# Channel mixing: five row blocks of 3, 3, 3, 4 and 4 tiles instead of four of 4, 4, 4 and 5

## What is computed

```python
    h2 = modulate(rms_norm(x), sh2, sc2)
    ff = jnp.square(jax.nn.relu(h2 @ w_up)) @ w_down
    x = x + g2[:, None, :] * ff
```

## Time and profile before

| | us |
|---|---|
| median of 3 runs | 3468.93 (3468.54 to 3474.66) |
| the profiled execution | 3469.96 |
| its span, first to last instruction | 3468.5 |
| stages ahead of channel mixing | up to 1902 |
| channel mixing, first block with its start | 1902 to 2274.6 |
| second, third block | 348.2, 348.3 |
| last block | 479.2 |
| tail behind the last matmul | 18.2 |

### The profile page before, as it was taken

The page is one execution under the profiler, slowest core; times in us unless marked ns, Lnnn a source line. Parts: engine busy times, 40 slices in busy tenths (PEclk is TensorE's granted clock), DMA queues, the critical chain, the costliest instruction groups (busy, mean ns, idle before and its releaser), DMA issues. The chain is left out here.

```text
span 3468.5 us, 50484 instructions
## 1 busy us (share of the span) xinstructions
PE 3159.5 (91%) x17260; PEld 2653.2 (76%) x17260; DVE 1988.9 (57%) x3373; ACT 1447.7 (42%) x2465; POOL 257.3 (7%) x262
## 2 busy tenths in 40 slices
PE   4999998579999999788697899999999999999997
PEld 2999997158877878555586688888888888888886
DVE  3656664558977879643465455565556555544444
ACT  2344343058877878533232333333333333222221
POOL 0000000111111111111000000020002000200001
PEclk7999999689999999898898899999999999999999
DMA  5567565853434341397776522253225222522211
GB/s 191 196 216 247 188 227 181 257 160 90 112 77 111 82 119 46 121 319 237 198 223 199 192 96 96 85 205 97 97 85 206 97 97 85 204 69 73 73 61 43
DMA packets 350196, 499.16 MB, mean 144 GB/s; under 512 B 24848, under 2 KB 282392, under 8 KB 343385
## 3 DMA queue, kind: packets, MB, share of 16 engines
q1 hardware_dynamic: 338253, 453.81, 41.8%
q0 software_dynamic: 11808, 43.79, 3.5%
HBM read 377.14 MB, written 107.95 MB: 140 GB/s over the span
## 5 line engine op out<-in xcount | busy, mean ns | idle before, releaser
L2285 PE MATMUL c_psu<-c_hT,c_up_hi 128*128 128x512 f32 x2048 | 677.3, 405 | 26.6 <-DVE c_up_lo L2209 19.3
L2230 DVE TENSOR_TENSOR c_ff<-c_ff,c_psd 128x512 f32<-128x512 f32 x544 | 365.8, 685 | 245.2 <-PE c_psd L2300 245.2
L2285 PEld LDWEIGHTS c_psu<-c_hT,c_up_hi 128*128 128x128 f32 x2048 | 386.5, 189 | 110.4 <-issue 19.7
L2300 PE MATMUL c_psd<-c_dn_hi,c_a_hi 128*128 128x512 f32 x1088 | 424.3, 390 | 0.0
L2300 PE MATMUL c_psd<-c_dn_hi,c_a_lo 128*128 128x512 f32 x1088 | 423.4, 389 | 0.0
L2300 PE MATMUL c_psd<-c_dn_lo,c_a_hi 128*128 128x512 f32 x1088 | 423.3, 389 | 0.0
L2285 PE MATMUL c_psu<-c_hT,c_up_lo 128*128 128x512 f32 x1024 | 414.1, 404 | 0.0
L632 PE MATMUL p_psm<-p_whi,p_hT_hi 128*128 128x384 f32 (+1 forms) x952 | 322.0, 338 | 17.0 <-DVE p_wlo L525 9.8
L2218 DVE TENSOR_TENSOR c_a_lo<-c_relu,c_a_hi 128x512 fp32r<-128x512 f32 (+1 forms) x128 | 92.7, 725 | 420.2 <-ACT c_a_hi L2176 420.2
L632 PE MATMUL p_psm<-p_whi,p_hT_lo 128*128 128x384 f32 (+1 forms) x952 | 316.1, 332 | 0.0
L632 PE MATMUL p_psm<-p_wlo,p_hT_hi 128*128 128x384 f32 (+1 forms) x952 | 311.8, 328 | 0.0
(11 more groups left out here) (235 smaller groups left out, 5530.2 us busy)
## 6 DMA issues: line engine op xcount, KB each, us to landing
c_up_raw<-in_w_up_dram SPq DMA_DIRECT2D x64, 1024.0 KB, 5.5
c_dn_raw<-in_w_down_dram SPq DMA_DIRECT2D x64, 1024.0 KB, 5.0
p_raw<-in_w_in_dram SPq DMA_DIRECT2D x24, 1536.0 KB, 7.5
s_krows<-in_cache_k_dram SPq DMA_DIRECT2D x16, 1536.0 KB, 6.6
s_vrows<-in_cache_v_dram POOLq DMA_DIRECT2D x16, 1536.0 KB, 7.6
o_wm<-in_w_mod_dram SPq DMA_DIRECT2D x16, 1024.0 KB, 7.1
q_split<-p_split SPq DMA_DIRECT2D x34, 384.0 KB, 2.3
k_split<-p_split SPq DMA_DIRECT2D x34, 384.0 KB, 2.4
```

The lines of the kernel that those rows point to most:

```text
L2230: dve.tensor_tensor(out, out, ps_d[bank_of(u, p, last)][:], ALU.add).then_inc(dn_free, 1)
L2285: done = pe.matmul(ps_u[g][:, 0, :], w[p][:, k, f], x[:, k, 0:RB], start=begin, stop=end)
L2300: done = pe.matmul(ps_d[bank_of(u, p, last)][:], a[p][:, g, rows], w[p][:, g, cols], start=(g == 0 and j == 0), stop=(g == G - 1 and j == 2))
```

## The change

Channel mixing takes its rows in five blocks: three of 3 tiles (SMALL = 3, NT = 3), then two of 4 (WT = 4), 17 tiles as before. The streams' tile is the fourth of the last block, inside its 512 columns. So an up matmul has one form per block, 384 or 512 wide, the 128-wide ones (and the second bank that they wrote) are gone, and relu is one instruction in every block. A block of three tiles has 6 units of down a step. The weights are loaded and split five times instead of four. The buffers hT, r, a_hi, a_lo, ff and x2 are 4 instead of 5 tiles wide. The first three blocks run in the hardware loop, the last two are written out. first_tile, units_before and bank_of are adapted; the bank of a unit starts over by parity of the step in the narrow blocks, since 6 is no multiple of 4. What each engine does in a step, and the order in which it does it, is otherwise as before.

The diff, cut to its core:

```diff
-    NB, RB = 4, 512
-    NT = RB // P
+    SMALL, NB = 3, 5
+    NT, WT = 3, 4
     G = 2
     STEPS = FF // P // G
     HALVES, W = 2, 512
     UNITS = NT * HALVES
-    LAST_UNITS = (NT + 1) * HALVES
+    WIDE_UNITS = WT * HALVES
     BANKS = 4
-    CREDIT = UNITS + 1
+    CREDIT = WIDE_UNITS + 1
...
-        ff = sb("c_ff", [P, NT + 1, D])
-        x2 = sb("c_x2", [P, NT + 1, D])
+        ff = sb("c_ff", [P, WT, D])
+        x2 = sb("c_x2", [P, WT, D])
...
-        ps_u = [ctx.enter_context(nc.psum_tensor(f"c_psu{i}", [P, 2, W], F32)) for i in range(G)]
+        ps_u = [ctx.enter_context(nc.psum_tensor(f"c_psu{i}", [P, W], F32)) for i in range(G)]
...
+        def first_tile(b, wide):
+
+            return WT * b - (WT - NT) * SMALL if wide else NT * b
+
+        def units_before(S, wide):
+
+            if wide and not (isinstance(S, int) and S < SMALL * STEPS):
+                return WIDE_UNITS * S - (WIDE_UNITS - UNITS) * SMALL * STEPS
             return UNITS * S
...
+        def bank_of(u, p, wide):
+
+            return (u + (0 if wide else UNITS * p)) % BANKS
 
         def over_blocks(eng, body):
 
-            with eng.Fori(0, NB - 1) as b:
-                body(b, False)
-            body(NB - 1, True)
+            with eng.Fori(0, SMALL) as b:
+                body(b, False, False)
+            for b in range(SMALL, NB):
+                body(b, True, b == NB - 1)
...
-                if last:
-                    act.activation(r[:, g, 0:W], ps_u[g][:, 0, :], ACT.Relu)
-                    act.activation(r[:, g, W:], ps_u[g][:, 1, 0:P], ACT.Relu).then_inc(relu_done, 1)
-                else:
-                    act.activation(r[:, g, 0:W], ps_u[g][:, 0, :], ACT.Relu).then_inc(relu_done, 1)
+                w = width(wide)
+                act.activation(r[:, g, 0:w], ps_u[g][:, 0:w], ACT.Relu).then_inc(relu_done, 1)
...
-                            done = pe.matmul(ps_u[g][:, 0, :], w[p][:, k, f], x[:, k, 0:RB], start=begin, stop=end)
-                            if last:
-                                done = pe.matmul(ps_u[g][:, 1, 0:P], w[p][:, k, f], x[:, k, RB:], start=begin, stop=end)
+                            done = pe.matmul(ps_u[g][:, 0:rows], w[p][:, k, f], x[:, k, 0:rows], start=begin, stop=end)
```

More of the change, by code:

```diff
@@ L2061, in _, with load_hT @@
         def _(sp):
-            def load_hT(b, last):
+            def load_hT(b, wide):
                 n = KT // PARTS
@@ L2067, in load_hT @@
                         src = t[name].rearrange("(k p) r -> p k r", p=P).bitcast(F32)
-                        w = width(last)
-                        cols = slice(b * RB, b * RB + w) if isinstance(b, int) else bass.ds(b * RB, w)
+                        w, first = width(wide), first_tile(b, wide) * P
+                        cols = slice(first, first + w) if isinstance(b, int) else bass.ds(first, w)
                         sp.dma_start(hT[i][:, k, 0:w].bitcast(F32), src[:, k, cols]).then_inc(hT_in[part], 16)
@@ L2139, in body @@
                     pool.memset(ff[:], 0.0).then_inc(zeroed, 1)
-                pool.wait_ge(y_stored, 16 * (NT * b + n))
+                pool.wait_ge(y_stored, 16 * (first + n))
                 if not last:
[L2142 to L2146, removed]
+                    load_x2(b + 1, next_wide)
+            with pool.Fori(0, SMALL - 1) as b:
+                body(b, False, False, False)
+            for b in range(SMALL - 1, NB):
+                body(b, b >= SMALL, True, b == NB - 1)
         @block.scalar
@@ L2213, in split_down, with rest @@
                 dve.tensor_tensor(dn_lo[p][:], dn_raw[:], dn_hi[p][:].bitcast(F32), ALU.subtract).then_inc(dn_ready, 1)
-            def rest(S, p, g, last):
-                w = width(last)
+            def rest(S, p, g, wide):
+                w = width(wide)
                 dve.wait_ge(a_hi_ready, G * S + g + 1)
@@ L2227, in accumulate, with weigh @@
                         dve.wait_ge(zeroed, b + 1)
-                    dve.wait_ge(dn_free, n - tiles(last) * HALVES + 1 + CREDIT)
+                    dve.wait_ge(dn_free, n - tiles(wide) * HALVES + 1 + CREDIT)
                     out = ff[:, u // HALVES, u % HALVES * W:(u % HALVES + 1) * W]
[L2230 to L2235, removed]
+                    dve.tensor_tensor(out, out, ps_d[bank_of(u, p, wide)][:], ALU.add).then_inc(dn_free, 1)
+            def weigh(S, wide, last, q):
+                dve.wait_ge(dn_free, units_before(S, wide) + (q + 1) * HALVES + CREDIT)
+                dve.tensor_tensor(ff[:, q, :], ff[:, q, :], gate[:, 1 if last and q == WT - 1 else 0, :], ALU.mult).then_inc(gated, 1)
             dve.sem_inc(dn_free, CREDIT)
@@ L2274, in _, with up @@
         def _(pe):
-            def up(S, p, last, block_start=None):
+            def up(S, p, wide, block_start=None):
+                rows = width(wide)
                 pe.wait_ge(up_ready, S + 1)
@@ L2299, in down @@
                         for j, (a, w) in enumerate(((a_hi, dn_hi), (a_hi, dn_lo), (a_lo, dn_hi))):
-                            done = pe.matmul(ps_d[bank_of(u, p, last)][:], a[p][:, g, rows], w[p][:, g, cols],
+                            done = pe.matmul(ps_d[bank_of(u, p, wide)][:], a[p][:, g, rows], w[p][:, g, cols],
                                              start=(g == 0 and j == 0), stop=(g == G - 1 and j == 2))
```

131 lines of the change are left out of this document (61 added, 70 removed).

## The result

The changed kernel takes 3441.89 us (median of 5 runs, 3436.81 to 3447.13), the kernel before 3468.54 us on the same chip (5 runs, 3462.31 to 3474.66). The ratio is 0.9928, 95% interval 0.9909 to 0.9946: 0.7% faster. The forecast was 3446 us and 3433 to 3456.

The account below looks back on a forecast made before the run. TensorE's matmul rate was taken to bound channel mixing; -31.1 steady, +8.8 boundaries, +1.5 clock, -1.6 start and -0.7 tail sum to -23.1 us, against the median 3445.8, forecast 3446 us, range 3433 to 3456.

Parts of the forecast that it names:

- The narrow matmul: Up product of the old last block: a 128-wide matmul costs 113.3 ns, half of a 512-wide one; 768 take 87.0 us.
- 55.8 ns: Price of a 128-wide matmul by the skill's N / 2.4 + 2.5 ns, by which up takes 706 us before and after.
- The steady sum: Steps of all blocks: 1523.7 us before, 1492.6 us after, -31.1 us, with a narrow step of 16.59 us.
- the rule "columns plus 13.3 ns": Lower bound for a 384-wide up matmul: 173.3 ns; as a rival it gave 3441 us, 12 in 100.
- The boundaries: Two boundaries between narrow blocks (0 to 1, 1 to 2): 4.3 to 4.4 us of waits each, +8.8 us.
- The mechanism: Behind a block's end: weighings, low weights, down load, ScalarE, first sum don't shrink; TensorE waits 1.1 and 3.2 us.
- The clock: Narrow boundaries: a 3.2 us wait may lower the granted clock; one of the two counted, +1.5 us (bounds 0 and 3).
- The start: First block: 1.57 MB less ahead of the down weights, 4.0 us; -1.6 us net (bounds 0 and -4).
- the step "9.9 us for the second up": First block: from up(1) on 9.9 + 8.2 us instead of 12.4 + 10.9, so up(2) starts 9.2 us earlier.
- The tail: Stage's end: the last block has four instead of five tiles to weigh, add and store, -0.7 us.
- Boundaries 2 to 3 and 3 to 4: Boundaries into the two wide blocks: no wait, 0 us.

Follow-up runs that it names:

- banks: The changed kernel with six instead of four PSUM banks for down in the narrow blocks: 3432.68 us, ratio 0.9892 to the kernel before.
- order on VectorE: The changed kernel with the low parts of the next weights made ahead of a block's last two weighings: 3435.32 us, ratio 0.9891 to the kernel before.

## Why the prediction was right, point by point

Set against the stage's 26.5 us (forecast 23.1):

- **The narrow matmul.** 113.3 ns was read from the distance in the alternating pair, and 112.8 were measured by leaving them out. That the price is not linear was the step on which the sign hung. The forecast sets 55.8 ns from the Trainium skill beside it; the section that it names, "Back-to-back issue gap", gives that formula for a matmul by itself, says that it comes out too low for narrow ones in a stream with their weight loads, and has about 81 ns there for 128 columns. So the distance from that page to this trace is 81 against 113 ns, not 55.8 against 113.
- **The steady sum.** Forecast -31.1 us, measured -33.2: 48 narrow steps of 16.55 us instead of 16.59. Two small errors against each other: a 384-wide matmul costs 173.8 ns, near the lower bound of 173.3 and not the 175.6 of the projection (4 us less), and a down matmul in a narrow step 227.8 instead of 226.7 ns (8.20 us for 36, 2 us more). Of the two rows I had for it I took the nearer in width; the rule "columns plus 13.3 ns" was the better one here.
- **The boundaries.** Forecast +8.8 us of waits and +1.5 of clock, 10.3 in all, measured 7.7. The trace shows 5.1 us of it as idle time (0.15 + 2.88 and 0.14 + 1.91). The low clock was there at the first boundary alone and cost about 1.6 us. Most of the last us lies in the stops themselves: a matmul is shown with an end 0.16 us behind the next one's start, so a stop costs 0.16 us more than its idle time, and there are four; the other 0.4 us is not assigned. The mechanism is the forecast one, link by link, and the two experiments that break it at different links (banks, order on VectorE) both remove it. The size was off by 1 us at the head of the chain. VectorE's last two weighings start 0.9 us behind the block's end (here the start of the next block's first matmul, 2184.5 us; 2274.6 before) instead of 1.4 and take 3.21 us instead of 3.76; all that follows took what was forecast (low parts 4.49 and 4.47 us, load 7.12), so the sum's bank came 25.6 us behind the block's end and not 26.6, and the wait was 0.15 + 2.88 us and not 1.1 + 3.2. The clock was right in sum by chance: one of two was counted, since shorter waits mostly wouldn't lower it, but in other executions waits of 2.67 and 2.88 us did each time, and in two executions both boundaries lost it. The row of the weighings:

```profile
2185.44 3.21 DVE L2233 TENSOR_TENSOR c_ff<-c_ff,c_gate 128x1024 f32<-128x1024 f32 x2
```

- **The start.** Forecast -1.6 us, measured +0.1. The load did land 3.8 us earlier (forecast 4.0). But the step "9.9 us for the second up" assumed the clock's loss of the kernel before; the first narrow up was through 5.5 us earlier, so the wait grew to 5.95 us, and the second up took 11.43 us. (In four other executions with the same loads ahead of it, it took 9.95 to 11.32 us behind waits of 4.41 to 6.09 us; so up to 1.5 us of this are the execution's.) A shorter block behind the same queue only waits longer, and here pays for it with the clock.
- **The tail.** Forecast -0.7 us, measured -0.8 (17.5 instead of 18.4 us from the start of the last matmul).
- Boundaries 2 to 3 and 3 to 4: no wait, as foretold; the fourth block's 348.1 us show it.

These sum to -33.2 + 7.7 + 0.1 - 0.8 = -26.2 us. The terms were off by -2.1, -2.6, +1.7 and -0.1 us: that the forecast is no further off than 3.1 us owes something to the start, whose error goes against the others. The forecast of 3446 us lies 4 us above the measured median; the stages ahead alone scatter by more.

## What to carry to other kernels

Don't count a narrow matmul by its columns: here 512, 384 and 320 columns cost their own time at 2.4 GHz plus 13 to 14 ns, but 128 columns cost 113 ns where that rule gives 67. No width between 128 and 320 was measured, and no run shows what sets the price of the narrow one. Cut a ragged width into equal parts instead of a full one and a rest: here 320 and 320 in place of 512 and 128 gave all that a fifth block gave, with no boundary to pay for. When steps get shorter, look at what doesn't shrink with them, which is the chain from the end of one block to the first result of the next: a spare buffer at its end or one operation fewer ahead of its head removes the wait. And when the scatter of other stages is as large as the effect, compare the length of the changed stage in several profiles.

## What the runs showed of the hardware

**The clock after a short wait.** The granted clock stayed up after waits of 1.69, 1.91 and 2.13 us, and fell from 1.0 to 0.5 after 2.67, 2.88 (in two executions), 3.17, 3.23 and 3.63 us. At the narrow boundaries, compared with those where it stayed up, the low clock cost 1.4 to 1.6 us after four of these waits and 2.7 to 2.8 us after those of 3.23 and 3.63, half to nearly nine tenths of the wait itself.

**The price of a matmul by its width.** At the full clock, each with its own weight load, the distance between starts is 226.7 ns for 512 columns, 173.8 for 384 (175.6 in the projection), 146.6 for 320 and 111 to 113 for 128. With the columns at 2.4 GHz taken off that leaves 13.3, 13.8 and 13.3 ns, and 58 to 60 for the narrow one.

**VectorE and GpSimd stand still for each other.** A subtraction of two SBUF tiles of 128x2048 takes 2.28 us on VectorE when GpSimd adds nothing, and 4.48 us where GpSimd's addition runs when it starts. The rows of the changed kernel, GpSimd first:

```profile
2187.75 3.16 POOL L2133 TENSOR_TENSOR c_x<-c_x,c_ff 128x1024 f32<-128x1024 f32 x1
...
2192.18 3.13 POOL L2133 TENSOR_TENSOR c_x<-c_x,c_ff 128x1024 f32<-128x1024 f32 x1
```

```profile
2188.58 4.49 DVE L2207 TENSOR_TENSOR c_up_lo<-c_up_raw,c_up_hi 128x2048 fp32r<-128x2048 f32 x1
2192.99 4.47 DVE L2211 TENSOR_TENSOR c_dn_lo<-c_dn_raw,c_dn_hi 128x2048 fp32r<-128x2048 f32 x1
```

GpSimd's additions end at 2190.91 and 2195.31; from there to the end of VectorE's subtractions it is 2.16 and 2.15 us, about one undisturbed duration. So VectorE did not run at half speed, it waited for GpSimd's instruction to end and then ran. The other way round, GpSimd's addition that starts at 2192.18, inside VectorE's, takes 3.13 instead of 2.4 us. The Trainium skill says this in "SBUF — State Buffer", section "Who interferes with whom": the port pair that the two engines share is an exclusive lock, and a VectorE instruction with two inputs in SBUF contends for it with a GpSimd instruction that reads SBUF. That the other engine stands still for the whole instruction it says of VectorE's two-port modes; for two inputs it is this trace that shows it. The Trainium skill also says there that a GpSimd instruction that only writes does not contend; the trace of the kernel before agrees, where a clearing by GpSimd runs from 2287.59 to 2291.99 and the two low parts of activations inside it, from 2288.45, take 1.28 us together, their usual time. In my forecast the 4.48 us stood as a given; the experiment on the order on VectorE showed that they are a choice.
